# Moving the turns between stages into the panels around them, with another schedule for the modulations

## What is computed

```python
def first_block(...):
    for l in range(2):
        mod = silu(c) @ w_mod[l] + b_mod[l]              # 2048 x 6144
        shift, scale, gate = split(mod, 3)
        h = x * (1 + scale) + shift
        y = diff_attention(h, ...) if l == 0 else forgetting_attention(h, w_q, w_out, k, v, F)
        # k, v, F = shared_kv(x, ...), with a modulation of its own (2048 x 4096)
        x = layer_norm(ALPHA * x + gate * y, ln_g[l], ln_b[l])

def second_block(x, ...):
    sh1, sc1, gt1, sh2, sc2, gt2 = silu(c) @ w_mod + b_mod   # 2048 x 12288
    x = x + gt1 * rmsnorm(s5_mixer(modulate(rmsnorm(x), sh1, sc1)))
    h = modulate(rmsnorm(x), sh2, sc2)
    x = x + gt2 * rmsnorm(square(relu(h @ w1)) @ w2)
```

## Time and profile before

| | |
|---|---|
| median of 3 runs | 2586.02 us (2583.11 to 2586.52) |
| the profiled execution's own time | 2586.52 us |
| its span on the core | 2584.7 us |
| mean granted TensorE clock | 0.945 |
| PE / DVE / ACT / POOL busy | 92% / 69% / 40% / 7% |
| DMA | 699.70 MB, mean 271 GB/s |

### The profile page before, as it was taken

The page is one execution under the profiler, slowest core; times in us unless marked ns, Lnnn a source line. Parts: engine busy times, 40 slices in busy tenths (PEclk is TensorE's granted clock), DMA queues, the critical chain, the costliest instruction groups (busy, mean ns, idle before and its releaser), DMA issues.

```text
span 2584.7 us, 41601 instructions
## 1 busy us (share of the span) xinstructions
PE 2378.9 (92%) x17407; PEld 1982.5 (77%) x17407; DVE 1789.7 (69%) x2871; ACT 1038.6 (40%) x1564; POOL 181.5 (7%) x290
## 2 busy tenths in 40 slices
PE   5699999999889899899999588999799999999998
PEld 1478887777666787698887385787798998998986
DVE  4648887988766676867888657777554677555545
ACT  0243334454542333434653222444444443443443
POOL 1102433011100000211000000000000000000000
PEclk7899999999899899999999758999899999999999
DMA  9969999697978599978678888688355687656552
GB/s 382 347 216 352 377 356 325 242 363 284 356 293 317 188 350 334 354 276 303 236 278 307 260 311 323 232 277 276 115 180 194 230 278 269 218 180 195 180 174 103
DMA packets 268363, 699.70 MB, mean 271 GB/s; under 512 B 13648, under 2 KB 14160, under 8 KB 246928
## 3 DMA queue, kind: packets, MB, share of 16 engines
q1 hardware_dynamic: 249344, 627.29, 69.3%
q0 software_dynamic: 18560, 67.66, 7.3%
q10 hardware_dynamic: 272, 2.10, 0.2%
HBM read 646.78 MB, written 56.49 MB: 272 GB/s over the span
## 4 chain that ended last, share of the span: by engine, by line
PE 70%; DVE 15%; DMA 10%; ACT 2%; issue 1%; SPq 1%; DVEq 0%; POOL 0%; ACTq 0%
PE bank L2305 69%; DVE ring_lo L1448 4%; DVE arena L1448 3%; DMA ring<-in_w_mod 3%; DVE sm L1448 2%; PE bank L2308 2%; DMA ring<-in_a_w_in 2%; DVE arena L1456 1%; DVE LT L1456 1%; DMA ring<-in_kv_w 1%; DMA ring<-in_b_w_out 1%; DMA m_state<-MSB 1%; DMA ring<-in_b_w_in 1%; DVE MSB L1448 1%; ACT att_w_hi L1040 1%
## 5 line engine op out<-in xcount | busy, mean ns | idle before, releaser
L1448 DVE TENSOR_TENSOR ring_lo<-ring,w_hi 128x1024 fp32r<-128x1024 f32 (+1 forms) x380 | 427.7, 1134 | 351.3 <-ACT w_hi L1040 333.5
L1040 ACT CAST w_hi<-ring 128x1024 fp32r<-128x1024 f32 x316 | 330.2, 1048 | 471.6 <-PE bank L2305 471.5
L1040 ACT CAST att_w_hi<-ring 128x1024 fp32r<-128x1024 f32 x192 | 196.7, 1048 | 324.8 <-DMA ring<-in_kv_w 124.1
L1448 DVE TENSOR_TENSOR ring_lo<-ring,att_w_hi 128x1024 fp32r<-128x1024 f32 x192 | 233.3, 1220 | 121.3 <-ACT att_w_hi L1040 120.0
L2305 PE MATMUL bank<-in_hi,w_hi 128*128 128x256 f32 x1024 | 290.2, 283 | 1.1 <-ACT n L987 1.1
L2305 PE MATMUL bank<-in_lo,w_hi 128*128 128x256 f32 x1024 | 290.1, 283 | 0.0
L2305 PE MATMUL bank<-in_hi,ring_lo 128*128 128x256 f32 x1024 | 289.7, 283 | 0.0
L2305 PE MATMUL bank<-w_hi,hid_lo 128*128 128x512 f32 x640 | 254.3, 397 | 0.4 <-DVE ring_lo L1448 0.4
L2305 PE MATMUL bank<-att_w_hi,att_hi 128*128 128x512 f32 x512 | 208.7, 408 | 14.7 <-DVE ring_lo L1448 14.7
L2305 PE MATMUL bank<-ring_lo,att_hi 128*128 128x512 f32 x512 | 202.7, 396 | 0.0
L2305 PE MATMUL bank<-w_hi,hid_hi 128*128 128x512 f32 x512 | 202.6, 396 | 0.0
(11 more groups left out here) (278 smaller groups left out, 5015.0 us busy)
## 6 DMA issues: line engine op xcount, KB each, us to landing
ring<-in_w_mod SPq DMA_DIRECT2D x192, 1024.0 KB, 9.1
ring<-in_a_w_in SPq DMA_DIRECT2D x64, 1024.0 KB, 9.6
ring<-in_w_mlp_in SPq DMA_DIRECT2D x64, 1024.0 KB, 5.2
ring<-in_w_mlp_out SPq DMA_DIRECT2D x64, 1024.0 KB, 5.1
ring<-in_kv_w_mod SPq DMA_DIRECT2D x32, 1024.0 KB, 9.9
ring<-in_kv_w SPq DMA_DIRECT2D x32, 1024.0 KB, 7.7
ring<-in_b_w_in SPq DMA_DIRECT2D x32, 1024.0 KB, 5.9
ring<-in_s_w_glu SPq DMA_DIRECT2D x32, 1024.0 KB, 5.3
```

Source lines behind the costliest of these rows:

```text
L1040: a.copy(whi(h), raw_half(h)).then_inc(*o.up("whi"))
L1448: return v.tensor_tensor(dst, x, y, op).then_inc(*(to or o.up("dve")))
```

## The change

1. The keys' and the MLP's turns use four banks, `GO = (2, 3, 5, 6)`. Six pairs are turned ahead of the panel (`TURNED_FIRST`), the last two behind the panel's halves r = 0 and 1. Scaling, rounding and remainder alternate quarter by quarter on ACT and DVE.
2. The queries' turn uses banks 5 and 6 and lies within panel 11: PE turns pair r behind half r, ACT and DVE do theirs behind the halves' `w_hi` and `w_lo` (`q_turn`). Only the last quarter is rounded ahead of panel 12. The scale is made ahead of panel 11.
3. The quad parts of panels 4 to 6 and modulation 32 (panel 7) are loaded and multiplied between the panel's own halves.
4. DVE's modulations begin at panel 6 instead of 8, none lies in panel 11 or at the MLP's turn, and they are denser in panels 12 to 19 (1.74 instead of 1.5 pieces per half) and 24 to 30 (1.14 instead of 1).
5. At the MLP's turn, DVE makes the first variance ahead of the last sum, and `w_hi`/`w_lo` of half 259 stand within the turn. PE turns the first four pairs' upper rows as soon as the first diagonal is there.

```diff
+TURN_BANKS = {"k": GO, "q": GC, "mlp": GO}
+TURNED_FIRST = 6
...
-QUAD_IN = {n: (6, range(4 * n, 4 * n + 4)) for n in range(4)}
+QUAD_IN = {n: (6 + n // 4, range(4 * (n + n // 4) % 16, 4 * (n + n // 4) % 16 + 4)) for n in range(7)}
+QUAD_OUT = {3: 6, 6: 7}
 FOUR_AT_LN = (7, range(4))
-FOUR_AT_STEP = {n: (7, range(4 * n - 12, 4 * n - 8)) for n in range(4, 7)}
-MOD_AT_STEP = {7: 32}
+MOD_IN = {7: 32}
...
-DVE_RUNS = [(8, 32, range(33, 37)), (12, 64, range(37, 43)), (20, 28, range(43, 46)), *((n, 16, (j,)) for n, j in
-            ((24, 48), (26, 49), (28, 50), (30, 51), (40, 52), (42, 53), (44, 54), (46, 55)))]
+DVE_RUNS = [(6, 36, range(33, 36)), (12, 92, range(36, 46)), (24, 56, range(48, 52)), *((n, 16, (j,)) for n, j in
+            ((40, 52), (42, 53), (44, 54), (46, 55)))]
...
+            def q_turn(i):
+
+                if i % 2:
+                    turned("q", i, h_raw["q"], sc1, M("m1", 0), 3)
+                elif i:
+                    turned_hi("q", AHk, h_raw["q"], i // 2 - 1)
...
-            def split_in(which, raw_, acol_, bcol_, n_scol, dst, first=8 * NS):
+            def split_in(which, raw_, acol_, bcol_, n_scol, dst, halves={}):
 
                 for k2 in turned_in(which, raw_, acol_, bcol_, n_scol):
-                    if k2 > 1:
-                        a.wait_ge(*emptied("xt", which, k2 - 3))
-                        own()
-                        in_hi(dst, raw_, k2 // 2 - 1)
-                        w_hi(first + k2 // 2 - 1)
-                a.wait_ge(*emptied("xt", which, 6))
-                own()
-                in_hi(dst, raw_, 3)
-                w_hi(first + 3)
+                    q = k2 // 2
+                    if q in halves:
+                        w_hi(halves[q])
+                    turned_hi(which, dst, raw_, q)
...
+                elif n == N_Q - 1:
+                    mod_bias("m1s")
+                    v.wait_ge(*emptied("xt", "k", 7))
+                    own()
+                    ts(sc1, M("m1", 16), 1.0, None, ADD, None, *o.up("scol"))
                 elif n == N_Q:
-                    v.wait_ge(*emptied("xt", "k", 7))
-                    v.wait_ge(*filled("step", N_Q - 1, 1))
-                    own()
-                    ts(sc1, M("m1", 16), 1.0, None, ADD, None, *o.up("scol"))
-                    split_in("q", h_raw["q"], sc1, M("m1", 0), AHk, ALk, N_Q)
+                    turned_lo("q", ALk, AHk, h_raw["q"], 3, N_Q)
...
             row_factors(aN, row_mix, "gsq", "mix", 5)
-            for i in range(4):
+            for i in range(3):
                 add_scaled(aN, i)
             x_var(0)
-            w_lo(8 * N_MLP + 3)
-            for j, k in PIECES[8 * N_MLP + 3]:
-                mod_piece(j, k)
-            x_factor(0)
+            add_scaled(aN, 3)
             mod_bias("m2d")
...
+                    if r % 2 and n in MOD_IN:
+                        if r == 1:
+                            quad_sums(N_QUADS - 1)
+                        mod_part(MOD_IN[n], r // 2)
+                    if r < 8 - TURNED_FIRST and n == N_K:
+                        turn_in("k", xv, (TURNED_FIRST + r,))
+                    if r < 8 - TURNED_FIRST and n == N_MLP:
+                        turn_scaled((TURNED_FIRST + r,))
+                    if n == N_Q - 1:
+                        turn_in("q", xv, (r,))
```

More of the change, by code:

```diff
@@ L172, in step @@
                 part(g, ks[q])
+            if n in MOD_IN:
+                ring.use(("mod", MOD_IN[n], q), slots)
+        if n in MOD_IN:
+            bank.use(("mod", MOD_IN[n]), GM)
         for b in range(2):
@@ L175, in step @@
         for r in range(8):
+            if n == N_Q - 1:
+                bank.use(("xt", "q", r), TURN_BANKS["q"])
             if n == N_K and r == 3:
@@ L729, in load_w @@
                         part(g, ks[q])
+                    if key[0] == "step" and key[1] in MOD_IN:
+                        j = MOD_IN[key[1]]
+                        load(("mod", j), MOD_W[MODS[j][0]], 0, 128 * MODS[j][1], q)
             def mod(j):
@@ L1003, in rsqrt, with turned, turned_hi @@
                 act(dst, tmp, ACT.Exp, *o.up("rs0"), scale=-0.5)
+            def turned(which, k2, dst, acol_, bcol_, n_scol):
+                a.wait_ge(*filled("xt", which, k2))
+                if k2 == 1:
+                    a.wait_ge(S["scol"], n_scol)
+                for j in range(2):
+                    k = 2 * k2 + j
+                    act(dst[:, k, :], bank("xt", which, k2)[:, 256 * j:256 * j + 256], ACT.Identity,
+                        *(empty("xt", which, k2) if j else o.up("act")), scale=acol_[:, k:k + 1], bias=bcol_[:, k:k + 1])
             def turned_in(which, dst, acol_, bcol_, n_scol):
                 for k2 in range(1, 8, 2):
[L1007 to L1013, removed]
-                    yield k2
+                    turned(which, k2, dst, acol_, bcol_, n_scol)
+                    yield k2
+            def turned_hi(which, dst, src, q):
+                a.wait_ge(*emptied("xt", which, 2 * q))
+                own()
+                in_hi(dst, src, q)
+            def q_turn(i):
[3 more added lines that the diff above has]
+                    turned_hi("q", AHk, h_raw["q"], i // 2 - 1)
             def bcast(which, dst, *part):
@@ L1334, in scalar_program @@
                     act(tz, tz, ACT.Ln, *o.up("zl"), bias=1.0)
[L1335 to L1340, removed]
+                if n in QUAD_OUT:
+                    quad(QUAD_OUT[n])
+                if n in MOD_IN:
+                    mod(MOD_IN[n])
             for n in range(N_W1, N_GLU):
@@ L1480, in newton, with turned @@
                 tt(dst, dst, tmp, MUL, *to)
+            def turned(which, k2, dst, acol_, bcol_):
+                v.wait_ge(*filled("xt", which, k2))
+                if k2 == 0:
+                    own()
+                for j in range(2):
+                    k = 2 * k2 + j
+                    ts(dst[:, k, :], bank("xt", which, k2)[:, 256 * j:256 * j + 256], acol_[:, k:k + 1], bcol_[:, k:k + 1],
+                       MUL, ADD, *(empty("xt", which, k2) if j else o.up("dve")))
             def turned_in(which, dst, acol_, bcol_):
                 for k2 in range(0, 8, 2):
-                    v.wait_ge(*filled("xt", which, k2))
-                    if k2 == 0:
-                        own()
[L1487 to L1490, removed]
+                    turned(which, k2, dst, acol_, bcol_)
                     yield k2
@@ L1509, in in_lo, with turned_lo, split_in, q_turn @@
                 tt(quarter(dst, q), quarter(src, q), quarter(hi_, q), SUB, *o.up("hlo"))
-            def split_in(which, raw_, acol_, bcol_, hi_, dst, n, first=8 * NS):
+            def turned_lo(which, dst, hi_, src, q, n):
+                v.wait_ge(*emptied("xt", which, 2 * q + 1))
+                in_lo(dst, hi_, src, q, n)
+            def split_in(which, raw_, acol_, bcol_, hi_, dst, n, halves={}):
                 for k2 in turned_in(which, raw_, acol_, bcol_):
                     if k2:
[L1514 to L1519, removed]
+                        q = k2 // 2 - 1
+                        turned_lo(which, dst, hi_, raw_, q, n)
+                        for i in ((0, 1), (2,), (3,))[q]:
+                            if i in halves:
+                                w_lo(halves[i])
+                turned_lo(which, dst, hi_, raw_, 3, n)
+            def q_turn(i):
+                if i % 2 == 0:
+                    turned("q", i, h_raw["q"], sc1, M("m1", 0))
+                elif i > 1:
+                    turned_lo("q", ALk, AHk, h_raw["q"], (i - 3) // 2, N_Q)
             def round_of(n, last=False):
@@ L2812, in tensor_program @@
                     bcast("mix", pcol)
-            turn_scaled()
+            turn_scaled(range(TURNED_FIRST))
             for n in range(N_MLP, NS):
```

81 lines of the change are left out of this document (37 added, 44 removed).

## The result

The changed kernel is slower, by less than half a percent. Median of 5 runs 2595.74 us (2591.41 to 2598.99) against 2586.52 us (2583.11 to 2588.79) for the kernel before on the same chip: ratio 1.0039, 95% interval 1.0027 to 1.005, so 7 to 13 us. The forecast was 2572, with a range of 2559 to 2582.

A forecast was written before the change was run, and what follows sets the result against it. PE bounds the kernel (70% of the span), so time is won where PE waits or runs slowly. Terms -1.6 + 11.7 - 17.3 - 2.5 + 0 + 2 - 7 = -14.7 us gave 2572 us, range 2559 to 2582.

The forecast's parts named there:

- The keys' turn: Before panel 4: first product 4.6 us earlier; with costs given back in panels 4 and 5, 1.6 us gained.
- The queries' turn: In panel 11: hidden by the products; panels 8 to 11 take 99 us, minus 17.3, and panel 12 starts near 1094.
- The MLP's turn: Before the MLP: first product 8.9 us earlier, minus 7 us after costs given back; turn about 20 us long.
- 10.7 loads of DVE for panels 8 to 11: Panels 8 to 11: DVE's loads there fall from 16 to 10.7, none of them in panel 11.
- The clock rival: Panel 11: transposes behind every half make the clock fall, giving 2575 to 2594 us; chance 0.03.
- between 3.6 and 14 I take 12: Panels 6 and 7: waits over PE's own time, from DMA load and held slots; panel 8 starts 10 us later.
- The cycle was priced at 8.9 us: Panels 6 and 7: load issue to slot given back takes 8.9 us, where PE needs 6.3.
- DVE gets 1.9 pieces more per panel ... I take +2: Panels 16 to 19: extra DVE pieces cost 1.5 us a panel, bounds 0 and 6, taken as +2 us.
- The lead stays 4.1 halves: 0: Panels 13 to 15: more loads but shorter holding leave the lead unchanged, cost 0, between -3 and +5 us.
- DVE's loads hold the slots in every panel: Rival: panels 13 to 15 lose roughly 7 us each, panels 6 and 7 lose 20, giving 2601 us; chance 0.07.
- The ring keeps up: Rival: panels 6 and 7 cost only the 3.6 us of DMA, giving 2564 us; chance 0.22.
- The queries' gain is drained later: Rival: panels 12 to 15 wait 7 us more, without the pause for DMA to catch up: 2579 us; chance 0.15.

The follow-up runs named there:

- number 10: Changed kernel, the four pieces of each VectorE modulation load bunched in one half from half 123 to 168: 2586.1 us, ratio 0.9995 to the kernel before.
- number 3: Changed kernel with modulations 36 to 45 put back to their earlier places and density, 33 to 35 left as changed: 2583.99 us, ratio 0.9982.
- number 9: Changed kernel with modulations 36 to 41 in halves 100 to 155 and 42 to 45 in 156 to 191, one load later: 2591.3 us, ratio 1.0009.
- number 4: Changed kernel with modulations 36 to 45 put back and 33 to 35 starting at half 68 (panel 8): 2573.67 us, ratio 0.9945.
- number 1: Kernel before with only the modulations moved as in the change, none of the three turns touched: 2615.41 us, ratio 1.0105.
- numbers 8, 9, 11 and 12: Changed kernel: 8 narrow pieces, short loads, 2587.0 us; 9 see number 9; 11 modulations 33-35 from half 64, 33-36 bunched, 2563.88; 12 also panels 12-14, 20 on bunched, 2555.73.

## Why the prediction was wrong

**The turns: right.** The keys' turn made panel 3 with it 4.5 us shorter (4.6 forecast), panel 4 took 42.5 us (43.4) and panel 5 27.6 (27.9). The queries' turn is hidden: panel 11 takes 25.83 us at clock 1.00 (just under the 26 to 28 forecast), panels 8 to 11 99.6 (99), and panel 12 runs at 1.00. Its starting time missed (1107.2 instead of 1094), because all ahead of it was later. The MLP's turn takes 21.0 us ("about 20"), though one step in it was off: the first diagonal's 16 records were not done when the second came, since PE works there at 1.2 GHz first, 0.21 us a record and not 0.16. The forecast's 10.7 loads of DVE for panels 8 to 11 are 8 by the table; nothing in the sum hung on them. And 0.9 us of what panel 12 gained are the sum of modulation 36, which no longer stands behind it but is made up for in panels 13 to 15.

The clock rival is gone too: 32 transposes lie in panel 11 at a clock of 1.00. (A transpose is one record in the trace here, not two: the panel's 130 records are 96 products, these 32 and 2 others.) The Trainium skill, TensorE: Matmul & The Clock Gate, Part 4, says that work in transpose mode does not count as busy in the same way. This row shows no fall of the clock by it, but it tests the rule weakly, since the transposes take some 3 of the 25.83 us and always stand between products.

**The step that failed: "between 3.6 and 14 I take 12".** The mechanism of panels 6 and 7 was the right one, but the term, forecast at 11.7 us against the kernel before, measured 20.3, above even its upper bound. Of waits there were 17.2 us, where 12 were taken, and the 3.2 us of lower clock that such waits bring had no term at all. The cycle was priced at 8.9 us: 5.1 to landing, then 3.8 for `w_hi`, `w_lo` and two pieces. In the chain three rounds of it go from 956.61 to 999.44, 14.3 each. Two terms were short. From landing to slot, 7.5 us and not 3.8: I had left out that VectorE, in its order, does the second half's `ring_lo` and a step of the scan before the last pieces. And the transfer took 11.85 us in one round, since a late slot in a ring of strict turns lets the loads behind it out together, here four of them; the 5.1 us I had used are a median over the MLP's loads.

**The second: "DVE gets 1.9 pieces more per panel ... I take +2".** I priced the pieces as work (1.5 us a panel) and had no term for the moment by which a sum needs its last piece. Panels 13 to 19 lost 11.5 us, 8.7 of them in panel 18, where PE stands 6.8 us at the sum of modulation 41 (number 10). "The lead stays 4.1 halves: 0" held better than the sum: panels 13 to 17 lost 2.5 us, 0.9 of them that sum of 36. Panels 20 to 30 I didn't price: 7.1 us more. 4.3 of them lie in panels 20 to 22 (86.8 us, 82.6 before) and go back to 83.0 in number 3 and 82.1 in number 9. The density is no cause for these, since it hardly changed there (1.71 pieces a half before) and is not lower in number 9; their cause and that of the rest stay open.

Together: 8.6 in panels 6 and 7, 9.5 in 13 to 19 and 7.1 in 20 to 30, less 3.5 by which the other terms came out better, is 21.7 us: from -14.7 to +7.

**The rivals.** "DVE's loads hold the slots in every panel" was the nearest: for panels 6 and 7 its cause is the one shown, and its 20 us are exact. It had 0.07. For the panels behind, it was wrong: panels 13 to 15 lost 2.4 us, not 21, and panel 18 has another cause. "The ring keeps up" (0.22) is refuted by the 76.4 us, where it had 59.4. "The queries' gain is drained later" (0.15) did not come either: panels 12 to 15 take 105.8 us, 106.9 before. Panel 14 alone is 4.6 us longer, 0.9 of them a sum that it didn't have before, at a DMA share of 0.99, and panel 15 is 2.4 shorter.

## What to carry to other kernels

In a ring with strict turns, price a load by how long its slot is held, and not by its bytes or its arithmetic: the same loads cost 20 us with their reads spread over three halves and 7 with the reads together. When a stage is moved forward, look at the deadlines that hang on it, and do the same when a table is made denser: a sum that comes at the end of the very round that makes its last piece costs the wait for all of that round (9.1 us in panel 10 of number 4, 6.8 in panel 18 of the change, and the clock on top). A change with two parts of opposite sign is worth taking apart before it is dropped: the turns were worth 17 us here, and with the loads rescheduled and bunched the whole is 33 us faster than before.

## What I had not expected of the hardware

Panel 0, which has the same instructions in all kernels, took 32.4 us in some profiled executions and 35.8 in others. In both, PE stands 2.9 us in the same place; what differs is the granted clock. The kernel before, and then the kernel of number 1, in the two stretches of 8 us that hold the pause and follow it:

```profile
743.00:751.00 8.00, 5.12 (x24) 4.06 (x23) 6.47 (x10) 4.37 (x5) 1.80 (x3) 1.00 1.03 420
751.00:759.00 8.00, 8.00 (x41) 5.33 (x44) 5.96 (x11) 2.00 (x2) 0.00 (x0) 1.00 1.01 416
```

```profile
743.00:751.00 8.00, 5.12 (x22) 3.63 (x15) 5.88 (x10) 4.37 (x5) 1.80 (x3) 0.70 1.03 417
751.00:759.00 8.00, 8.00 (x35) 5.58 (x34) 6.20 (x10) 2.10 (x2) 0.00 (x0) 0.87 1.00 413
```

PE is busy the same 5.12 of 8 us, and the clock is 1.00 and 1.00 in one and 0.70 and 0.87 in the other: 3.4 us with no difference in the program there. The first line of the table of stretches, 5.5 us, is of this kind too: numbers 8, 9, 11 and 12 have the changed kernel's code up to panel 3 and reach it at 813.8 to 814.9 us, not at 820.2. A difference of that size in one panel of one execution is no evidence.
